# Queries in reverse order, one stored copy of the bias vector, and two weight chunks issued ahead of the bias transfers

## The reference, cut to what matters

```
h = rms_norm(x, norm_mix_g)
proj = h @ w_in                                   # 1024 x 7168
xr, gr, q, k, v, gates = split(proj)
y_rnn = rglru_branch(xr, gr, ...)                 # conv of width 4, block-diagonal gates, scan, gelu
# attention, 8 heads, two softmaxes a head, blocks of 128 queries:
bias = rel_table[rel_bucket(q_pos, k_pos)]        # a function of q_pos - k_pos and the head
s = einsum(q, k) * 64 ** -0.5 + bias ; masked where k_pos > q_pos
w = softmax(s[0]) - lam * softmax(s[1])
y_att = rms_norm(w @ v, subln_g) * (1 - lam_init)
x = x + (gates0 * (y_rnn @ w_proj_rnn) + gates1 * (y_att @ w_proj_att)) @ w_out
x = x + moe_ffn(rms_norm(x, norm_ffn_g), ...)     # top 4 of 32, clamped SwiGLU
return rms_norm(x, norm_final_g)
```

## Time and profile before

| | |
|---|---|
| median of 3 runs | 1339.21 us (1338.64 to 1341.05) |
| span of the profiled execution | 1338.2 us |
| PE busy | 1246.2 us (93%) |
| DVE, ACT, POOL busy | 262.6, 229.1, 10.6 us |
| moved | 453.01 MB, mean 339 GB/s |
| TensorE clock granted, mean over the span | 0.990 |

### The profile page before, as it was taken

How to read it: one execution, slowest core, us unless ns; L and a number is a source line. 1 busy time by engine, 2 the same in 40 slices (tenths; PEclk the granted TensorE clock), 3 DMA queues, 4 the chain that set the end, 5 groups by cost and what they waited for, 6 DMA issues and landing times.

```text
span 1338.2 us, 14530 instructions
## 1 busy us (share of the span) xinstructions
PE 1246.2 (93%) x5484; PEld 558.5 (42%) x5484; DVE 262.6 (20%) x573; ACT 229.1 (17%) x466; POOL 10.6 (1%) x20
## 2 busy tenths in 40 slices
PE   7499999999899999989899999999898999999996
PEld 6358888886433333323232323223232323232332
DVE  4300745152411111111111111111111111111112
ACT  3023334100201111111111111111111111111113
POOL 1000000000000000000000000000000000000000
PEclk9799999999999999999999999999999999999998
DMA  7733663465399999999999999999999999999994
GB/s 197 179 137 126 251 252 126 157 224 181 142 351 409 410 410 410 410 410 409 410 410 410 410 410 410 410 410 410 409 410 410 410 410 410 410 410 410 409 409 158
DMA packets 132924, 453.01 MB, mean 339 GB/s; under 512 B 10588, under 2 KB 12742, under 8 KB 132902
## 3 DMA queue, kind: packets, MB, share of 16 engines
q1 hardware_dynamic: 132902, 452.71, 87.1%
HBM read 450.06 MB, written 2.62 MB: 338 GB/s over the span
## 4 chain that ended last, share of the span: by engine, by line
SPq 52%; PE 35%; DMA 5%; issue 4%; DVE 3%; ACT 1%; ACTq 0%
SPq L307 49%; PE bank L1053 13%; PE bank L1217 13%; PE bank L1059 4%; DMA w_down_sb<-in_w_in 3%; SPq L346 2%; DMA w_up_sb<-in_w_up_e 1%; DVE arena L824 1%; PE bank L1332 1%; DMA w_down_sb<-in_w_out 1%; SPq L358 1%; PE bank L1089 1%; PE bank L1106 0%; PE bank L1231 0%; DVE arena L743 0%
## 5 line engine op out<-in xcount | busy, mean ns | idle before, releaser
L1217 PE MATMUL bank<-w_down_sb,arena 128*64 128x512 f32 x1024 | 238.4, 603 | 40.1 <-DMA w_down_sb<-in_w_down_e 39.5
L1217 PE MATMUL bank<-arena 128*64 128x512 f32 x1032 | 243.3, 598 | 0.0
L1217 PE MATMUL bank<-w_up_sb,arena 128*64 128x512 f32 x1024 | 235.7, 598 | 7.5 <-DMA w_up_sb<-in_w_up_e 7.1
L1053 PE MATMUL bank<-arena,w_down_sb 128*128 128x256 f32 x1024 | 225.8, 382 | 2.4 <-DMA w_down_sb<-in_w_in 1.2
L1053 PEld LDWEIGHTS bank<-arena,w_down_sb 128*128 128x128 f32 x1024 | 195.0, 191 | 30.6 <-DMA w_down_sb<-in_w_in 1.6
L1217 PEld LDWEIGHTS bank<-w_down_sb,arena 128*64 128x64 f32 x1024 | 68.7, 137 | 205.8 <-issue 128.4
L1217 PEld LDWEIGHTS bank<-w_up_sb,arena 128*64 128x64 f32 x1024 | 67.7, 136 | 148.7 <-issue 120.3
L1217 PEld LDWEIGHTS bank<-arena 128*64 128x64 f32 x1032 | 71.4, 137 | 135.4 <-issue 135.4
L1217 PE MATMUL bank<-w_gate_sb,arena 128*64 128x512 f32 x512 | 116.7, 598 | 0.0
L991 DVE TENSOR_SCALAR arena<-bank 128x512 f32<-128x512 f32 x32 | 22.1, 692 | 315.2 <-PE bank L1217 315.2
L988 DVE TENSOR_TENSOR arena<-arena 128x512 f32<-128x512 f32 x32 | 22.1, 692 | 301.7 <-ACT arena L617 301.7
(11 more groups left out here) (225 smaller groups left out, 574.6 us busy)
## 6 DMA issues: line engine op xcount, KB each, us to landing
w_up_sb<-in_w_up_e SPq DMA_DIRECT2D x128, 1024.0 KB, 18.2
w_down_sb<-in_w_down_e SPq DMA_DIRECT2D x128, 1024.0 KB, 18.4
w_gate_sb<-in_w_gate_e SPq DMA_DIRECT2D x64, 1024.0 KB, 18.0
arena<-in_w_gate_e SPq DMA_DIRECT2D x64, 1024.0 KB, 18.5
w_down_sb<-in_w_in SPq DMA_DIRECT2D x14, 2048.0 KB, 8.8
w_down_sb<-in_w_proj_rnn SPq DMA_DIRECT2D x2, 2048.0 KB, 8.1
w_down_sb<-in_w_proj_att SPq DMA_DIRECT2D x2, 2048.0 KB, 7.7
w_down_sb<-in_w_out SPq DMA_DIRECT2D x2, 2048.0 KB, 8.9
```

The costliest lines, as they stand in the source:

```text
L1053: ins = eng.matmul(ps[:, n * T:(n + 1) * T], w[:, k, (2 * b + n) * P:(2 * b + n + 1) * P], rhs[:, k, :], start=(k == 0), stop=(k == KC - 1))
L1217: ins = eng.matmul(ps[b * JB:(b + 1) * JB, :], lhsT, w[:, h * CH:(h + 1) * CH], **flags)
```

## The change

Queries are kept in reverse order of position: ACT writes q with a step of -1 along the positions, so column j holds query 255 - j. With partition p standing for query 127 - p of a block, its bias row is element p onwards of the vector, so all partitions can read one stored copy, each one element further than the last. The store writes 8 x 384 values; the scratch tensor has that size. The score and value matmuls take the other half of the columns, and the copy into `oT` turns the order back. On SP chunk 2 goes ahead of the wait for `bias_vec`, and chunk 3 ahead of the wait for the store.

```diff
-        head_size = P * (DIFFS + 1)
-        scratch = nc.dram_tensor("bias_scratch", (H, head_size), F32, kind="Internal").ap()
+        scratch = nc.dram_tensor("bias_scratch", (H, DIFFS), F32, kind="Internal").ap()
@@ SP
+            chunk(2)
             eng.wait_ge(s["bias_vector_ready"], 1)
-            eng.dma_start(scratch.rearrange("h (q m) -> h q m", q=P)[:, :, 0:DIFFS],
-                          bias_vec.rearrange("h (a m) -> h a m", a=1).to_broadcast([H, P, DIFFS])
-                          ).then_inc(s["bias_vector_stored"], 16)
-            chunk(2)
+            eng.dma_start(scratch[:, :], bias_vec).then_inc(s["bias_vector_stored"], 16)
+            chunk(3)
             eng.wait_ge(s["bias_vector_stored"], 16)
-            back = bass.AP(scratch.tensor, scratch.offset + P - 1, [[DIFFS, P], [head_size, H], [1, T]])
-            eng.dma_start(tb[:, :, :], back).then_inc(s["bias_tile_loaded"], 16)
+            shifted = bass.AP(scratch.tensor, scratch.offset, [[1, P], [DIFFS, H], [1, T]])
+            eng.dma_start(tb[:, :, :], shifted).then_inc(s["bias_tile_loaded"], 16)
...
-            for i in range(3, len(STREAM)):
+            for i in range(4, len(STREAM)):
@@ ACT, unit_out and head_out
-                    eng.activation(qz[0][0:HD, f:f + 2, :], halves(ps)[0:HD], ACT.Copy, scale=HD ** -0.5)
-                    ins = eng.activation(qz[1][HD:P, f:f + 2, :], halves(ps)[HD:P], ACT.Copy, scale=HD ** -0.5)
+                    eng.activation(qz[0][0:HD, f:f + 2, ::-1], halves(ps)[0:HD], ACT.Copy, scale=HD ** -0.5)
+                    ins = eng.activation(qz[1][HD:P, f:f + 2, ::-1], halves(ps)[HD:P], ACT.Copy, scale=HD ** -0.5)
...
-                eng.activation(oT[:, h, :], bank[6][:, 0:T], ACT.Copy
+                eng.activation(oT[:, h, ::-1], bank[6][:, 0:T], ACT.Copy
@@ PE, scores and head
-                    eng.matmul(bank[2 + h % 2][:, n * T:(n + 1) * T], qz[n][:, h, P:T], kT[:, h, :],
+                    eng.matmul(bank[2 + h % 2][:, n * T:(n + 1) * T], qz[n][:, h, 0:P], kT[:, h, :],
...
-                    ins = eng.matmul(bank[4][:, n * P:(n + 1) * P], qz[n][:, h, 0:P], kT[:, h, 0:P], start=True, stop=True)
+                    ins = eng.matmul(bank[4][:, n * P:(n + 1) * P], qz[n][:, h, P:T], kT[:, h, 0:P], start=True, stop=True)
...
-                eng.matmul(bank[6][:, 0:P], v[0], wT[:, 0:P], start=True, stop=True)
-                eng.matmul(bank[6][:, P:T], v[0], wT[:, P:T], start=True, stop=False)
-                eng.matmul(bank[6][:, P:T], v[1], wT[:, T:T + P], start=False, stop=True
+                eng.matmul(bank[6][:, P:T], v[0], wT[:, 0:P], start=True, stop=True)
+                eng.matmul(bank[6][:, 0:P], v[0], wT[:, P:T], start=True, stop=False)
+                eng.matmul(bank[6][:, 0:P], v[1], wT[:, T:T + P], start=False, stop=True
```

## The result

Beside four runs of the kernel before (median 1338.93 us), the changed kernel's four runs had a median of 1318.75 us (1316.83 to 1319.14). The recorded ratio is 0.9839, 95% interval 0.9826 to 0.9852; the two medians by themselves are 20.2 us apart, a quotient of 0.9849, near the upper end of that interval. The profiled execution took 1316.83 us with a span of 1315.1, 23.1 less than the profiled span before.

A forecast was written before the change was run, and what follows sets the result against it. The prediction took PE's wait ahead of v, for chunk 2 held behind the 1.5 MB store, as the bound. Wait -17.64 and clock -1.93 sum to -19.57 us: from 1339.21 to 1319.6 us, range 1317.5 to 1324.5.

The forecast's parts named there:

- step 2 (chunk 2): Weight chunk ahead of v's products: lands by 37.9 to 42.9 us, so v starts at 43.66 without PE's 17.64 us wait.
- Step 1 (store): Store to the scratch tensor: 1.5 MB become 12 KB, issued after chunk 2 and taken as done by 40 us.
- Step 3 (clock in v): PE's first unit of v: without the pause the granted clock stays at 1.00, gaining 1.93 us more.
- Step 4 (chunk 3): Weight chunk for v's third unit: issued at 43.7, lands at 51.8 to 56.8, before its need at 57.4; hidden.
- Step 5 (bias tile): Bias tile load, all partitions reading the same 12 KB: cost taken as 0, with 17.6 us of queue time free.
- third rival: Bias tile's 1024 rows served one after the other from the shared 12 KB: about 224 us slower, about 1563; chance 3%.
- Step 6 (steps of -1): ACT's reversed q writes and the copies into oT: cost taken as 0; 1.5 us if q's writes took four times as long.
- Step 7 (does it reach the end): Everything behind v: waits for units, not a time, so the whole gain of 19.57 us reaches the end.
- my own sign of being wrong: Prediction wrong if v starts later than 44 us, or the stretch from there to the end changes by over 2 us.
- A (no gain): Gain lost behind a later wait, the expert weight stream being at a bandwidth limit: 1338 to 1340 us; chance 2%.
- C (slower): The bias tile's shared rows are served one by one, delaying chunk 4: about 224 us slower, about 1563; chance 3%.
- B (a later wait): Chunk 3 or 4 becomes the next wait, part of the gain remains: 1321 to 1324 us, or 1334.6; chance 10%.

The follow-up runs named there:

- Experiments 2: The changed kernel with SP's old order (small store, then chunk 2, wait for the store, bias tile, chunk 3): 1318.7 us in the median.
- experiment 4: The kernel before, old order, same 128 copies (1.5 MB) written DRAM to DRAM from a 12 KB copy, copies as outer dimension: 1315.94 us, one execution.
- experiment 1: The kernel before with only SP's new order, the store keeping its 1.5 MB: 1334.25 us in the median, ratio 0.9966 to before.
- a1: The changed kernel run again with nothing changed, first of three repetitions: 1319.64 us in the median, ratio 0.9849.
- a3: The changed kernel run again with nothing changed, third of three repetitions: 1318.35 us in the median, ratio 0.984.
- experiment 3: The kernel before, old order, with 64 stored copies instead of 128, each read by two partitions in two tile loads: 1328.78 us, ratio 0.9918.

## Why the prediction was right or wrong

- *What bounds, and step 2 (chunk 2).* Right. PE went from xr to v with no wait (the chain); 17.6 us gone. Experiments 2 and 4 pin it on the store: take away its length in either way, with the old order, and the wait goes (4 in one execution).
- *Step 1 (store).* Right in the effect. I read "some 7 of 16 engines" from the trace and then reckoned with the volume alone; experiment 4 shows that the same volume does no harm when it is written with a share of about 1 in 12.6 us.
- *Step 3 (clock in v).* Right: v takes 27.47 us instead of 29.36 (1.89 against 1.93), its last copy starts at 71.00 against the 71.14 worked out. From the end of xr's first 32 products to v's end the change took off 19.57 us, which is the sum to the hundredth; that it is so exact is partly luck.
- *Step 4 (chunk 3).* Right; landing 8 us, no wait ahead of v's third unit.
- *Step 5 (bias tile).* Right at zero. The third rival, one row after another, is refuted by the 5.1 us; no rate was lost either. The rule on row pitch that I weighed from the Trainium skill ("DMA: Bandwidth & Descriptors", section "Latency and other measured facts") is about streams a large power of two apart; rows 4 bytes apart don't behave so here (5.1 us against 5.6). Even the 17 us that I had worked out from it were within my own slack of 17.6, so they were no ground for the third rival's chance.
- *Step 6 (steps of -1).* Right: 0.59 and 0.37 us, as before; 1.09 us of idle ahead of the k unit against 1.10.
- *Step 7 (does it reach the end).* This is the step that failed, by its size. "Every step behind v waits for units, not for a time", and so I put the change of everything behind v at nothing. It does pass the gain on. But my own sign of being wrong came true: from v's start to the end the profile after is 5.3 us shorter, 1.9 of them step 3's, so 3.4 us where I had allowed 2; and SP's wait for the job table was 15.2 us, not 16.7. The part behind v contains stretches whose length the program does not fix: 1.7 us in the last job and 1.2 to 1.5 around the router (4.1 in experiment 1), by the clock that the execution happens to be granted. The profile of before, my only one, had a slow clock at both, the first one after at neither; a1 and a3 came back to within 0.8 us of before. Against the one profile of before, the part behind v was 0.5 to 3.4 us shorter in the four of the changed kernel, 2.0 in the mean. The missing term is the mean of this part in either kernel, which one profile cannot give, and its spread. Ahead of the changed part xr's first products add up to 2 us of the same kind. The sum of 19.57 was exact for the front; the runs together say 20.8 with 1.2 of uncertainty, the first ratio 21.6. Over all runs the excess of 1.2 us is as large as its uncertainty.
- *How the numbers follow.* The range had its low end at 1317.5 from three runs of before (1338.64 to 1341.05). 31 runs show 1334.97 to 1343.45; four of the 17 runs after are under that low end. A range of 1315 to 1323 would have been honest for one execution.
- *Rivals.* A (no gain) and C (slower) did not happen. B (a later wait) did not happen in this kernel; it is what experiment 1 makes, where the store is left long.

What stays open: whether the 1.2 us of the 20.8 that are not in the sum are real, and if so, whether the kernel before meets the low clock behind the router more often (it was profiled once); the slow chunk 2 of experiment 3; what decides the clock around the router.

## What to carry to other kernels

When a transfer is long, look at its share of the engines before its bytes: a store at a share of 0.45 lasted 32.6 us and let the weight chunk behind it land after 31.4 us, and either fewer bytes (12 KB) or the same bytes at a share near 1 made it harmless, while moving it one place back in the queue mainly moved the wait. Work out a gain stage by stage, and then ask which other stages of that one profile had a low granted clock: those microseconds come and go by the execution, and only several profiles of the unchanged kernel price them. For a gain of 1.6%, the sum over the changed part was right to 0.1 us while single runs of one kernel differed by up to 8.5.

## What the runs showed of the hardware

- A load of 128 partitions x 8 rows of 1 KB out of one 12 KB area, each partition's rows 4 bytes on from the last's, landed in 5.1 us; with 1536 bytes from partition to partition it landed in 5.6 us (one transfer each).
- ScalarE's copies with a step of -1 in the output took what they took with +1: 0.59 us for 64 x 512, 0.37 us for 128 x 256 (0.36 before).
- 128 copies of 12 KB took 32.6 us from 8 partitions (share 0.44 to 0.45 alone) and 12.6 us from DRAM to DRAM with 128 as the outer dimension (share 1.09 alone, 0.93 over the 12.6 us with a chunk behind them).
- In one and the same program the granted clock fell or stayed after pauses of 1.15 and 0.69 us, with four transposes between them: 8.81 us at 0.81 or 7.11 us at 1.00 for the same 32 products.
- The recorded granted clock can be 1.00 at the start of an execution while the products take the slow time: 652 ns each against 385 in another execution.
